# The last product of a two-block network as Strassen's seven block products, its weight sums made on VectorE

## The reference

```python
    h = rmsnorm_2(x, ffn_norm_g[l])
    x = x + (jax.nn.silu(h @ w_gate[l]) * (h @ w_up[l])) @ w_down[l]
return rmsnorm_2(x, final_norm_g)
```

## Time and profile before

| | us |
|---|---|
| median of 3 runs | 1211.54 |
| span of the profiled execution, first to last instruction | 1209.1 |
| one feed-forward unit, from one to the next | 21.76 |
| transposes at the head of the last product | 3.60 |
| the last product's matmuls, first to last | 119.90 |
| from there to the end of the span | 6.20 |

### The profile page before, as it was taken

The page is one execution under the profiler, slowest core; times in us unless marked ns, Lnnn a source line. Parts: engine busy times, 40 slices in busy tenths (PEclk is TensorE's granted clock), DMA queues, the critical chain, the costliest instruction groups (busy, mean ns, idle before and its releaser), DMA issues.

```text
span 1209.1 us, 15625 instructions
## 1 busy us (share of the span) xinstructions
PE 1188.8 (98%) x5810; PEld 990.9 (82%) x5810; DVE 629.7 (52%) x1459; ACT 561.4 (46%) x1009; POOL 499.3 (41%) x277
## 2 busy tenths in 40 slices
PE   9999999999999999999999999999999999999997
PEld 8878778888888887799878788788888888888886
DVE  5789864774628264999964773954222231220002
ACT  6453574476522364557765785434322332221114
POOL 1428462345433424123252883444344434443441
PEclk9999999999999999999999999999999999999999
DMA  8204662302332523153123204322332333323211
GB/s 276 81 25 142 173 175 70 105 1 71 122 105 70 186 94 105 35 176 108 36 40 94 81 23 153 103 93 84 105 105 70 105 105 103 102 74 122 104 70 70
DMA packets 80618, 119.71 MB, mean 99 GB/s; under 512 B 16024, under 2 KB 42776, under 8 KB 80160
## 3 DMA queue, kind: packets, MB, share of 16 engines
q1 hardware_dynamic: 80544, 118.71, 30.3%
HBM read 108.20 MB, written 4.21 MB: 93 GB/s over the span
## 4 chain that ended last, share of the span: by engine, by line
PE 80%; DVE 11%; ACT 2%; POOL 2%; issue 2%; DMA 2%; SPq 1%; DVEq 0%; ACTq 0%; POOLq 0%
PE bank L1794 59%; PE bank L2112 9%; PE bank L1858 2%; PE bank L1890 2%; PE bank L1872 2%; PE bank L1936 2%; DVE sc L1472 2%; DVE m L1468 1%; DVE sqS L1618 1%; POOL w_lo L731 1%; PE bank L1834 1%; DMA rot<-in_rot 1%; PE bank L1975 1%; DVE rp L1218 1%; ACT w_hi L834 0%
## 5 line engine op out<-in xcount | busy, mean ns | idle before, releaser
L714 POOL TENSOR_TENSOR w_lo<-w_raw,w_hi 128x2048 fp32r<-128x2048 f32 (+3 forms) x78 | 352.0, 4513 | 584.9 <-ACT w_hi L802 527.6
L1794 PE MATMUL bank<-aH,w_hi 128*128 128x512 f32 x832 | 331.6, 399 | 2.6 <-DVE mqT L1669 1.1
L1794 PE MATMUL bank<-aH,w_lo 128*128 128x512 f32 x832 | 324.9, 391 | 0.0
L1794 PE MATMUL bank<-aL,w_hi 128*128 128x512 f32 x832 | 318.2, 391 | 0.0
L802 ACT ACTIVATE w_hi<-w_raw 128x2048 fp32r<-128x2048 f32 (+3 forms) x74 | 138.4, 1870 | 262.1 <-PE bank L1794 159.5
L1794 PEld LDWEIGHTS bank<-aH,w_hi 128*128 128x128 f32 x832 | 157.0, 189 | 33.5 <-issue 4.7
L1794 PEld LDWEIGHTS bank<-aL,w_hi 128*128 128x128 f32 x832 | 156.3, 188 | 33.4
L1794 PEld LDWEIGHTS bank<-aH,w_lo 128*128 128x128 f32 x832 | 156.9, 189 | 27.8 <-issue 0.2
L1218 DVE TENSOR_TENSOR fg<-bank,rB 128x512 f32<-128x512 f32 x22 | 15.1, 691 | 128.2 <-PE bank L1794 128.2
L1794 PE MATMUL bank<-uH,w_hi 128*128 128x512 f32 x192 | 75.0, 391 | 0.3 <-DVE uL L1690 0.2
L1794 PE MATMUL bank<-uL,w_hi 128*128 128x512 f32 x192 | 74.8, 390 | 0.0
(11 more groups left out here) (337 smaller groups left out, 2124.2 us busy)
## 6 DMA issues: line engine op xcount, KB each, us to landing
w_raw<-in_w_in SPq DMA_DIRECT2D x21, 1024.0 KB, 5.0
w_raw<-in_w_gate SPq DMA_DIRECT2D x22, 512.0 KB, 3.9
w_raw<-in_w_up SPq DMA_DIRECT2D x22, 512.0 KB, 4.8
w_raw<-in_w_down SPq DMA_DIRECT2D x11, 1024.0 KB, 4.8
w_raw<-in_w_merge SPq DMA_DIRECT2D x8, 1024.0 KB, 4.9
w_raw<-in_w_out SPq DMA_DIRECT2D x8, 1024.0 KB, 4.9
w_raw<-in_w_ple_gate SPq DMA_DIRECT2D x4, 1024.0 KB, 4.9
w_raw<-in_w_in SPq DMA_DIRECT2D x4, 512.0 KB, 7.2
```

The costliest lines, as they stand in the source:

```text
L714: pool.tensor_tensor(out=w_lo[:, c % 2, 0:n], in0=w_raw[:, c % 2, 0:n], in1=w_hi[:, c % 2, 0:n].bitcast(F32), op=ALU.subtract).then_inc(w_ ...
L1794: ins = pe.matmul(o, l, r, start=(kk == 0 and operand == ROUNDED and m == 0), stop=(kk == total - 1 and operand == REST), skip_group_check ...
```

## The change

The left operand (512 x 2816) is cut into two token halves and the weights into two column halves, and the 22 row tiles are taken in eleven pairs. A pair gives a 2 x 2 by 2 x 2 block product, which Strassen's form (in Winograd's order of sums) makes with seven block products in place of eight. Four of the seven (`p1`, `p6`, `p5`, `p4`) are accumulated over the eleven pairs in a first pass and three (`p2`, `p7`, `p3`) in a second; each has two banks, one for each of its token blocks. `p2`, `p7` and `p3` go on in the banks of `p1`, `p6` and `p5`, after these have been copied or added out.

- Each chunk of `w_down` is loaded twice: 1 MB in the first pass, its three needed quarters in the second (0.75 MB, two loads). There are three raw buffers (both halves of `w_raw`, and `third_raw`) and three pairs of split buffers (the two of `w_hi`/`w_lo`, and four tiles of `aH`/`aL`).
- DVE makes the sums of weight blocks in place (`down_sums`): three instructions of 128 x 512 for a chunk in the first pass, one in the second, one chunk ahead. ACT makes the high part (`down_high`), DVE the low part (`down_low`). POOL has nothing left to do after `f10`.
- The left operand's sums are made by DVE in the units (`operands`: one instruction of 128 x 512 and six of 128 x 256, three of them linked). The operands of the first pass are split in the units for `f0` to `f8` (`first_high`, `first_low`, 128 x 1024 each), and for the last two within the last product; those of the second pass (`last_high`, `last_low`, 128 x 768) within the last product.
- The transposes of the residual move into `f0` (16 before and 16 after its last two tiles), ACT copies them out (`x_turned`), and they go to DRAM and come back as `xr` (2 MB each way). The block products are added to `xr` by DVE.
- The end takes the token blocks in the order 2, 3, 0, 1. Each half is added into `xr` before it is squared.

```diff
-    unit("down", DFF, 2, [("w_down_2", 0, D)])
...
+FIRST_FOUR = (("p1", 1, 0), ("p6", 3, 3), ("p5", 2, 1), ("p4", 0, 2))
+LAST_THREE = {"p2": (2, 2), "p7": (1, 1), "p3": (0, 3)}
...
+    fill("xt", [4, 5, 6, 7] * 2)
...
-    fill("down", list(range(8)))
+    for product, banks in (("p1", (4, 5)), ("p6", (6, 7)), ("p5", (0, 1)), ("p4", (2, 3)),
+                           ("p2", (4, 5)), ("p7", (6, 7)), ("p3", (0, 1))):
...
+            for d in range(STEPS):
+                if d == 0:
+                    wait_filled(sp_, "xt", 7)
+                elif d < 3:
+                    sp_.wait_ge(w_hi_ready, n_chunks - 2 + d)
+                    sp_.wait_ge(w_lo_ready, n_chunks - 2 + d)
+                else:
+                    sp_.wait_ge(down_lo, d - 2)
+                raw = down_raw(d)
+                if d < PAIRS:
+                    sp_.dma_start(raw.rearrange("p (k n) -> p k n", n=D), pair_of(d)).then_inc(down_landed[d % 3], 16)
...
+                if d == 7:
+                    sp_.wait_ge(tok_stored, 16)
+                    sp_.wait_ge(down_used, 4)
+                    sp_.dma_start(xr[:].rearrange("p b d -> p (b d)"), tok_dram).then_inc(tok_back, 16)
...
+            def first_high(j):
...
+                act.wait_ge(ff_done, j + 1)
+                act.activation(first_hi[first_slot(j)][:], first_raw(j)[:], ACT.Copy).then_inc(first_split_hi, 1)
...
+            def down_high(d):
...
+                    down_done(act, d - 2)
+                act.wait_ge(down_summed, d + 1)
+                at = slice(0 if d < PAIRS else S, CH)
+                act.activation(down_part(0, d)[:, at], down_raw(d)[:, at], ACT.Copy).then_inc(down_hi, 1)
...
-                for j in range(2):
-                    t = 2 * f + j
-                    act.wait_ge(ff_prod, t + 1)
-                    act.activation(fH[:, t, :], fg[:, j, :], ACT.Copy).then_inc(ff_hi, 1)
...
+            for f in range(PAIRS - 1):
+                ahead(f"f{f}")
+                if f == 0:
+                    x_out(0)
+                    x_out(1)
+                silu(f)
+                if f < EARLY:
+                    first_high(f)
+            ahead(f"f{PAIRS - 1}")
+            for d in range(3):
+                down_high(d)
+            for d in range(3, PAIRS):
+                down_high(d)
+                if d == 4:
+                    silu(PAIRS - 1)
+                if d == 5 or d == 6:
+                    first_high(EARLY + d - 5)
+                if d >= 7:
...
+            def sums_into(w11, w12, w21, w22):
+                link(minus(w12, w12, w11))
+                link(minus(w22, w22, w12))
+                return minus(w21, w21, w22)
+            def down_sums(d):
+                dve.wait_ge(down_landed[d % 3], down_landed_by(d))
+                w11, w12, w21, w22 = (down_raw(d)[:, S * i:S * i + S] for i in range(4))
+                if d < PAIRS:
+                    sums_into(w11, w12, w21, w22).then_inc(down_summed, 1)
+                else:
+                    minus(w12, w22, w12).then_inc(down_summed, 1)
...
+            def operands(f):
+                raw = first_raw(f)
+                wait_emptied(dve, f"f{f}", 2)
+                dve.wait_ge(ff_act, 2 * f + 1)
+                mult(raw[:, 1:3, :].rearrange("p q t -> p (q t)"), fg[:, 0, :], fu[:, 0, :])
+                wait_emptied(dve, f"f{f}", 3)
+                dve.wait_ge(ff_act, 2 * f + 2)
+                mult(last_raw[:, f, 2, :], fg[:, 1, 0:HT], fu[:, 1, 0:HT])
+                link(mult(raw[:, 0, :], fg[:, 1, HT:S], fu[:, 1, HT:S]))
+                link(plus(raw[:, 2, :], raw[:, 2, :], raw[:, 0, :]))
+                link(minus(raw[:, 3, :], raw[:, 2, :], raw[:, 1, :]))
+                minus(last_raw[:, f, 0, :], last_raw[:, f, 2, :], raw[:, 3, :])
+                minus(last_raw[:, f, 1, :], raw[:, 0, :], raw[:, 3, :]).then_inc(ff_done, 1)
+            for f in range(PAIRS - 1):
+                gates_out(f)
+                if f == 0:
+                    for i in range(8):
+                        wait_filled(dve, "xt", i)
+                operands(f)
+                if f < EARLY:
+                    first_low(f)
+            down_sums(0)
+            down_sums(1)
+            down_low(0)
+            gates_out(PAIRS - 1)
+            down_low(1)
+            for d in range(2, PAIRS + 2):
+                if d == 2:
+                    down_sums(d)
+                down_sums(d + 1)
+                down_low(d)
+                if d == 4:
+                    operands(PAIRS - 1)
+                if d == 6 or d == 7:
+                    first_low(EARLY + d - 6)
+                if 7 <= d < PAIRS:
+                    last_low(d - 7)
...
+            def fin_add(n):
+                b, i = (n + 2) % NB, n % 2
+                for half, at in enumerate((low_at, high_at)):
+                    product = "p7" if n < 2 else ("p2", "p3")[half]
+                    wait_filled(dve, product, i)
+                    plus(xr[:, b, at], bank_of(product, i)[:], xr[:, b, at]).then_inc(fin_sum, 1)
...
+            for d in range(PAIRS):
+                pe.wait_ge(down_lo, d + 1)
+                pe.wait_ge(first_split_lo, d + 1)
+                for name, q, w_at in FIRST_FOUR:
+                    hi, lo = first_hi[first_slot(d)][:, q, :], first_lo[first_slot(d)][:, q, :]
+                    for i in range(2):
...
+            for d in range(PAIRS, STEPS - 3):
+                pe.wait_ge(down_lo, d + 1)
+                pe.wait_ge(last_split_lo, d - PAIRS + 1)
+                for name in ("p2", "p7", "p3"):
+                    for i in range(2):
+                        ins = last(name, i, d)
+                ins.then_inc(down_used, 1)
+            for i in range(2):
+                for d in range(STEPS - 3, STEPS):
+                    pe.wait_ge(down_lo, d + 1)
+                    pe.wait_ge(last_split_lo, d - PAIRS + 1)
+                    ins = last("p7", i, d)
+                fills(ins, "p7", i)
+            for i in range(2):
+                for name in ("p2", "p3"):
+                    for d in range(STEPS - 3, STEPS):
+                        ins = last(name, i, d)
+                    fills(ins, name, i)
```

More of the change, by code:

```diff
@@ L585, in w_view, with down_raw, down_part, down_landed_by @@
             return buf[:, c % 2, 0:per * n].rearrange("p (k n) -> p k n", n=n)
+        n_chunks = len(CHUNKS)
+        def down_raw(d):
+            return third_raw[:, :] if d % 3 == 0 else w_raw[:, (n_chunks + d % 3 - 1) % 2, :]
+        def down_part(part_, d):
+            if d % 3 == 2:
+                return (aH, aL)[part_][:, 0:4, :].rearrange("p k t -> p (k t)")
+            return (w_hi, w_lo)[part_][:, (n_chunks + d % 3) % 2, :]
+        def down_landed_by(d):
+            return sum(16 if i < PAIRS else 32 for i in range(d % 3, d + 1, 3))
+        def down_done(eng, n):
+            if n == PAIRS:
+                wait_filled(eng, "p4", 1)
+            else:
+                eng.wait_ge(down_used, n if n < PAIRS else n - 1)
+        def pair_of(d):
+            k = 2 * (d % PAIRS)
+            return dram["w_down_2"][0, k * P:(k + 2) * P, :].rearrange("(k p) n -> p k n", p=P)
+        def first_slot(j):
+            return j if j < EARLY else j - EARLY
+        def first_raw(j):
+            return later[0] if j < EARLY else later[j - EARLY]
         landed, total = [], [0, 0]
@@ L1187, in _ @@
+            for n in range(NB):
+                b = (n + 2) % NB
                 for half in range(2):
-                    i = 2 * b + half
-                    wait_filled(act, "down", i)
-                    act.activation(sq[:, half, :], bank_of("down", i)[:], ACT.Square,
+                    act.wait_ge(fin_sum, 2 * n + half + 1)
+                    act.activation(sq[:, half, :], xr[:, b, S * half:S * half + S], ACT.Square,
                                    accum_out=qs[:, half, b:b + 1]).then_inc(fin_sq, 1)
-                act.wait_ge(fin_bias, b + 1)
@@ L2089, in _ @@
                     spread(5)
+                    turn_x(0)
+            turn_x(1)
             for f in range(1, DFF // 256):
                 gemm(f"f{f}", aH, aL, False)
-            for i in (4, 5, 6, 7, 0, 1, 2, 3):
-                b, half = i // 2, i % 2
-                o = open_bank("down", i)
-                for j in range(4):
-                    pe.matmul(o[:, j * P:(j + 1) * P], xT[:, 4 * half + j, b * P:(b + 1) * P], ident[:], start=(j == 0), stop=False,
-                              is_transpose=True, skip_group_check=True)
@@ new lines, in last @@
+            def last(name, i, d):
+                q, w_at = LAST_THREE[name]
+                j = d - PAIRS
+                if d == PAIRS:
+                    open_bank(name, i)
+                return product(name, i, d, last_hi[j % 4][:, q, :], last_lo[j % 4][:, q, :], w_at, False, d == STEPS - 1)
+            for d in range(PAIRS, STEPS - 3):
+                pe.wait_ge(down_lo, d + 1)
```

(5 more changed lines are left out.)

205 lines of the change are left out of this document (151 added, 54 removed).

## The result

The changed kernel takes 1213.8 us (median of 20 runs, 1210.45 to 1217.41), the kernel before 1210.61 (20 runs, 1209.68 to 1212.94): 3.2 us more, a ratio of 1.0027 with a 95% interval of 1.0021 to 1.0034. It is slower: the interval lies above 1. The forecast was 1209.7; it started from 1211.54, the median of three runs, which is 0.9 above that of the 20. Of all executions in this document one, of x5_fill2, is left out: it took 1965.21 us at a mean granted clock of 0.56.

A forecast was written before the change was run, and what follows sets the result against it. PE was taken as the bound (80% of the chain of waits). -15.0 for fewer matmuls, +6.4, +2.8, +0.4, +2.4 and +1.2 for waits and the end gave -1.8: 1211.5 to 1209.7 us, range 1203 to 1215.

The forecast's parts named there:

- 66 matmuls fewer: Last product: 462 matmuls on PE against 528, at 0.2267 us each, -15.0 us.
- waits in f2 to f9: Units f2 to f9: PE waits 0.8 us for w_lo at each second chunk, +6.4 us.
- f0 and f1: Chain of copies, table load and splits after f0 takes 15.5 us against PE's 12.7; PE waits in f1, +2.8 us.
- chunks of the first pass: Product's first pass: DVE's low parts 2 and 5 each 0.2 us late, +0.4 in the sum.
- wait for the last chunk: Product's last three chunks: last buffer freed late, 3.8 us to prepare against six matmuls (1.4) on PE, +2.4 us.
- the end behind PE: Last scaling ends 4.0 us behind PE in place of 2.85, as DVE adds both halves before squaring, +1.2 us.
- a fixed 2.4 above the profiled span: Whole kernel: the runs' median was taken to stay 2.4 us above the profiled span.
- I take 0 for it, with 1 us as the other end: Product's middle: xr's return, queued ahead of chunk 8, lands that chunk at about 33 us; DVE ready at 32.7.
- the units hold: Rival, units: the 9.2 us of waits fall away, 1200.5 us, or about 1205 if half do; chance 0.22.
- the ring of loads: Rival, product's first pass: slow loads hold DVE, 6.1 us a chunk, nine give +6.2, 1216 us; chance 0.20.
- no overlap on DVE: Rival, units: DVE instructions spaced by full length, 0.26 us more a unit, +2.3, 1212.0 us; chance 0.08.

The follow-up runs named there:

- x5_fill2: Changed kernel plus eight matmuls filling PE's wait ahead of chunk 21 and eleven filling its wait in unit f1: 1211.2 us.
- x1_units: Changed kernel with ACT making w_hi of the next unit's second chunk before first_high: 1201.19 us, ratio 0.993.
- x4: Changed kernel with the return of xr queued behind chunk 10 instead of 7 and gfin's reload behind chunk 15 instead of 8: 1211.99 us.
- x6: The changed kernel once more, no edit, with a second profile: 1214.72 us, ratio 1.003.
- x11: Changed kernel with only gfin's reload (0.5 MB) moved behind chunk 15, run once: 1213.14 us.
- x9: The same kernel as x5_fill2, run again for its profile: 1211.91 us, ratio 1.0006.
- x12_xr: Changed kernel with only the return of xr (2 MB) moved, from behind chunk 7 to behind chunk 10, run once: 1208.90 us.
- x3: Changed kernel plus eight matmuls into an unread bank, filling PE's wait ahead of chunk 21: 1212.17 us, ratio 1.0011.
- x8: Changed kernel with w_hi before first_high, chunk 21 behind 18 matmuls, xr and gfin loads later, an unused root before the end's first square: 1198.96 us.

## Why the prediction was wrong

Term by term, on the profiled execution, in us:

| term | forecast | measured |
|---|---|---|
| 66 matmuls fewer | -15.0 | -15.0 |
| waits in f2 to f9 | +6.4 | +6.7 (1060.25 - 879.48 = 180.77, against 8 x 21.76) |
| f0 and f1 | +2.8 | +3.1 |
| chunks of the first pass | +0.4 | +1.7 |
| wait for the last chunk | +2.4 | +2.3 |
| half clock behind it | none | +1.6 |
| the end behind PE | +1.2 | +1.2 |
| start of f0, stores | 0 | +0.2 |
| sum | -1.8 | +1.8 |

(f0 and f1: the second chunk of f1 began at 872.92 before, eight units ahead of 1047.00, and begins at 879.48; off that go 0.1 that f0 starts later and 3.3 for the transposes, which are no longer between f10 and the product.)

The mechanism was right: PE's saved time is spent on `w_lo` in the units, and x1_units, which mends that order alone, gives back 12.6 us in the median; 9.7 of the 12.4 in its profile are the units. But the saving was forecast to outweigh its price by 1.8, and the span grew by 1.8. Two steps failed.

The first is the sum itself: it prices every wait at its length and the matmuls behind it at 0.2267. In unit f10 and the product, whose stretches were read the earlier trace rows, PE never stood still and the clock was 1.00. The wait of 2.0 us brings 1.6 us of half clock in this execution and in x4, x6 and x11; that of f1 brings the same in three of seven. It fits this that the executions spread, and that the median lies 1.4 us further from the one before than the two profiled spans do (the profiled one has no half clock in f1); no run measures that part by itself. Filling both waits, with their length unchanged, takes back 1.9 to 2.6 us of the 3.2 (x5, x9). The trace of before had the fall of the clock, at 575, in a stage that the prediction did not look at, though not its price. Nor does the median lie a fixed 2.4 above the profiled span, as the sum took it to: it lies 2.9 above it after the change, and over 20 runs 1.5 above it before.

The second is "I take 0 for it, with 1 us as the other end", for the return of `xr`. The estimate of when DVE is ready was right; that the 1 MB behind `xr` adds 3.0 us was not. `xr` landed 30.1 us after the product's first matmul, which leaves 33 for chunk 8, but chunk 8 landed at 34.4, 4.3 later: DVE waits 1.6 (1.7 to 3.0 in other executions with the units unchanged), and PE 1.3 us more than forecast. x12_xr, where only this load moves, has none of it.

The rivals: of the first (the units hold) nothing is seen. The second (the ring of loads) is seen at one place, chunks 7 and 8, but one load was late, not all, and it costs 1.3 and not 6.2. The third (no overlap on DVE) falls: in the changed kernel two 256-column instructions of 0.42 start 0.33 apart (1050.07 and 1050.40), as two of 512 columns do with 0.61 for 0.69, and `operands` took 3.67 for the 3.66 forecast, where the lengths alone give 3.88. (The prediction's "3.62" does not fit its own 3.66, so its 0.26 a unit is 0.22, and its 2.3 is 2.0.) The rule that the prediction cites from the Trainium skill (VectorE: DVE Perf Modes, The DRAIN you can't avoid) is only a part of what stands there: the section also says that a next instruction that is not held starts earlier. The trace agrees with that, by 0.33 for 0.42.

What stays open: why the half clock comes in some executions and not in others behind the same wait. The profiles that have it in f1 all have it near 576 and at the end as well; none of the runs here varies what decides it.

## What to carry to other kernels

Where a change makes PE wait, look in the trace of before for a wait of about that length and read the granted clock behind it: the matmuls after the wait can cost nearly as much as the wait itself, in some executions only. What that is worth depends on whether PE has to wait soon after in any case: some 1.6 us at two places here, 0.5 at most at the third. In the order of an engine, put what PE waits for ahead of what only the next stage needs; here one line was worth four times the whole change in the other direction. And a load that is needed late should not be queued ahead of one that a full engine is about to need.

## What the runs showed of the hardware

- Behind PE standing still for 2.0, 2.3 and 2.7 us the granted clock fell to its lower level for some 4 us, in 4 of 6, 8 of 13 and 3 of 7 profiles. This cost 1.5 to 1.6 us behind the first and the third wait, and 0.5 at most behind the second, where PE waits again soon after. Behind waits of 1.55 and 1.60 us it stayed at 1.00 (x1, x9). Matmuls into a free bank in the wait kept it at 1.00 (x3, x9).
- Beside a `w_lo` on POOL a DVE subtraction of 256 columns took 4.70 us in place of 0.42, ending 0.3 after it, and `w_lo` took 0.2 longer (x1).
- The table load took 1.28 us for silu and for the root alike, and an unused root of one value (0.20 us) ahead of time was enough to have the table there (x8).
